# A two-block transformer on one core: index scores placed among the second queries' products, four last weight parts and a residual load moved, and the PSUM banks of some phases exchanged

## The chip, the cores and the metric

The kernel runs on one core of one Trainium2 chip. Its engines are TensorE (PE, with its weight loads shown apart as PEld), VectorE (DVE), ScalarE (ACT), GpSimd (POOL) and SyncE (SP, which only issues transfers here). The metric is the device time of one execution in microseconds, lower is better. A profile is a second kind of run: one execution recorded by the hardware profiler.

## The reference, cut to what matters

For 512 tokens of width 1024, all in float32, two blocks follow each other:

```python
# first block
z = rms_norm(x, norm1_g) @ w_in                       # glu_in, q, k, v, gate_logits
a = silu(rms_norm(conv31(a_val * sigmoid(a_gate)) + b, g));  y_a = a @ w_conv_out
o = mix over three dilated windows of softmax attention(q, k, v);  y_b = o @ w_attn_out
x = x + (g_a * y_a + g_b * y_b) @ w_out               # the residual is the input x
h = rms_norm(x, norm2_g)
u = conv3(h @ w_up);  x = x + (silu(u_gate) * u_val) @ w_down
# second block, first layer (sparse attention)
q, k, v, g, qi, wi, ki = split(x @ w_in_a)
rel = relu(einsum('qhd,sd->qhs', rope(qi), rope(ki)) * 64 ** -0.5)   # 8 index heads
score = einsum('qhs,qh->qs', rel, wi * 8 ** -0.5);  idx = top_k(score, 128)
x = layer_norm(ALPHA * x + (softmax attention over idx * silu(g)) @ w_out_a)
# second block, second layer (stick-breaking attention), then layer_norm
```

The index scores decide which keys a query sees: for each of three blocks of 128 queries (the first block needs no choice) and each of 8 index heads there is one product with a width of 256, 384 or 512 keys, a relu, and a weighted sum into a mask.

## The kernel before

**Weights.** All weight matrices stand in one stream of 231 slabs of 512 KB (`wstream`), in the order in which TensorE uses them (`PHASES`). A slab lies in one of four slots and is held in two parts, `W_HI` (rounded to the fast float32 format) and `W_LO` (the remainder). POOL does this (L422 to L440): for each slab it waits until the slab four places back is used up (`slab_done`), issues the load of `W_HI`, and then calls `remainder` for the slab before: negate `W_HI` into `W_LO` (L430), and issue a load that adds the original weights onto it (L433). `W_LO` is what TensorE waits for. For some early slabs ACT does the negation.

**Products.** Every product of 128 x 128 by 128 x 512 is three matmuls, high by high and two crosses (L451 to L453). A slab is 24 such matmuls. `f_phase` gives features by tokens, one PSUM bank per slab; `t_half` gives tokens by features, four slabs into four banks at once. Before it starts it waits until `tile_free` has counted enough tiles that were read out of PSUM. `tokens=` at the end of a phase makes the last two slabs of the half go token by token, so that both must be there when the first token's products run. `aside=` puts other work between slabs.

**Order of the work.** The program of each engine is written out by hand and every engine is strictly in order. TensorE goes through: the GLU projection (`glu`), the first q, k, v (`qkv`, L812), four early gate slabs, the rest of v, the convolution's output, attention "a" with the gate slabs as filling, `attn_out`, `w_out`, `up`, `down`, the index projection (`idx`), the second queries (`q2`, L853 to L859), and then as a block of its own: five turns of the index values (L868), and 24 score products (L877), where score `u` waits until the relu of score `u - 4` is done. After that come the second k and v (`kv2`), attention "b", `out_a`, and the last layer.

**Around the index scores.** ACT copies the index values out of PSUM, turns, copies the second queries (L945), copies the turned index values (L1205), and takes the 24 relus (L1212). DVE rotates the index values, and for each score adds the weighted relu onto `MASK` (L1747), then chooses the largest 128 of a row in 16 rounds, and rotates the second q and k.

**The residual of `w_out`.** `RESIDUAL` is a view of `GATE_B`. SP loads x into it again (L412) as one transfer of 2 MB, when all tiles of `attn_out` are free; DVE adds the products of `w_out` onto it.

## Time and profile before

| | us |
|---|---|
| median of 3 runs | 1651.69 (1646.33 to 1653.17) |
| the profiled execution | 1649.88 |
| its span | 1648.1 |
| TensorE busy in the span | 1561.9 (95%) |
| VectorE busy | 886.0 (54%) |
| ScalarE busy | 504.5 (31%) |
| GpSimd busy | 546.1 (33%) |
| weight stream, share of the 16 DMA engines | 68.7% |

The page cuts the span into 40 slices of some 41 us. TensorE is at 90% or more in nearly all of them. The transfers are at 80% to 90% of the DMA engines wherever TensorE goes through slabs without attention between them, and at 20% to 30% in the attention stretches. The chain of work that ended last lies on TensorE for 86% of the span. What is idle on TensorE adds up to some 5% in stretches of one to three microseconds.

### The profile page before, as it was taken

To read this page: it belongs to the slowest core of one execution; us is meant where nothing else is said; L and a number is where in the kernel's file an instruction comes from. 1 tells how busy PE (TensorE), PEld (TensorE's weight loads), DVE (VectorE), ACT (ScalarE), POOL (GpSimd) and SP (SyncE) were. 2 spreads that over 40 slices of the span, in tenths; PEclk is the share of its full clock that TensorE was granted. 3 is DMA by queue.
4 is the path that set the end of the run, shared out by engine and by line. 5 is a ranking of instruction groups with operands and counts; after the bars stand their busy time and mean duration, and the time that the engine had idled before them with its cause. 6 is when DMAs were issued, how large, how long until landed. Compare 5 with 4: busy or idle time off the path is not lost.

```text
span 1648.1 us, 19418 instructions
## 1 busy us (share of the span) xinstructions
PE 1561.9 (95%) x7634; PEld 1273.9 (77%) x7634; DVE 886.0 (54%) x1546; ACT 504.5 (31%) x1001; POOL 546.1 (33%) x662
## 2 busy tenths in 40 slices
PE   6999999899899999999999999999998989999997
PEld 5878888677778778888878787687776768888885
DVE  2899949256645144333400031895676261677675
ACT  4223333356541132222200011311676130444440
POOL 3222234311114344444444444144110334332321
PEclk9999999999999999999999999999999999999999
DMA  8989998623338978898888888398321758755655
GB/s 227 193 184 194 195 191 188 153 66 63 77 77 183 225 169 193 191 198 190 196 172 192 184 176 194 78 189 182 77 52 26 164 120 193 156 123 117 140 109 145
DMA packets 69274, 253.12 MB, mean 154 GB/s; under 512 B 7616, under 2 KB 7744, under 8 KB 69184
## 3 DMA queue, kind: packets, MB, share of 16 engines
q0 software_dynamic: 66528, 242.25, 68.7%
q1 hardware_dynamic: 2112, 7.53, 1.3%
q10 hardware_dynamic: 544, 2.10, 0.4%
q8 instruction: 61, 1.00, 0.3%
q14 instruction: 29, 0.24, 0.0%
HBM read 249.75 MB, written 2.10 MB: 153 GB/s over the span
## 4 chain that ended last, share of the span: by engine, by line
PE 86%; DVE 5%; DMA 3%; ACT 3%; issue 2%; POOL 0%; SPq 0%; DVEq 0%; ACTq 0%; POOLq 0%
PE PSUM L451 26%; PE PSUM L452 25%; PE PSUM L453 25%; DMA W_LO<-wstream 2%; PE PSUM L612 2%; PE PSUM L633 2%; PE PSUM L714 1%; PE PSUM L732 1%; PE PSUM L745 1%; PE PSUM L600 1%; DVE MASK L1747 1%; DMA SMALLS<-small 1%; DMA W_HI<-wstream 1%; PE PSUM L643 1%; ACT PROBS L968 0%
## 5 line engine op out<-in xcount | busy, mean ns | idle before, releaser
L439 POOL DMA_DIRECT2D W_HI<-wstream x231 | 129.5, 561 | 946.8 <-PE PSUM L453 946.3
L451 PE MATMUL PSUM<-X_HI,W_HI 128*128 128x512 f32 x872 | 350.0, 401 | 5.7 <-DVE X_LO L1332 2.6
L452 PE MATMUL PSUM<-X_LO,W_HI 128*128 128x512 f32 x872 | 342.1, 392 | 0.0
L453 PE MATMUL PSUM<-X_HI,W_LO 128*128 128x512 f32 x872 | 342.0, 392 | 0.0
L433 POOL DMA_DIRECT2D W_LO<-wstream x231 | 208.0, 900 | 105.2 <-POOL W_LO L430 84.2
L451 PE MATMUL PSUM<-W_HI,X_HI 128*128 128x512 f32 x544 | 213.8, 393 | 7.0 <-DMA W_LO<-wstream 2.7
L430 POOL TENSOR_SCALAR W_LO<-W_HI 128x1024 fp32r<-128x1024 f32 x195 | 210.3, 1079 | 23.1 <-DMA W_HI<-wstream 19.6
L452 PE MATMUL PSUM<-W_LO,X_HI 128*128 128x512 f32 x544 | 212.8, 391 | 0.0
L453 PE MATMUL PSUM<-W_HI,X_LO 128*128 128x512 f32 x544 | 212.7, 391 | 0.0
L451 PEld LDWEIGHTS PSUM<-X_HI,W_HI 128*128 128x128 f32 x872 | 165.0, 189 | 44.8 <-issue 7.5
L453 PEld LDWEIGHTS PSUM<-X_HI,W_LO 128*128 128x128 f32 x872 | 164.7, 189 | 35.8
L452 PEld LDWEIGHTS PSUM<-X_LO,W_HI 128*128 128x128 f32 x872 | 165.1, 189 | 32.0
L1597 DVE SCALAR_TENSOR_TENSOR CONV<-CONV_IN,SMALLS,CONV 128x512 f32<-128x512 f32 x240 | 159.4, 738 | 0.0
L1691 DVE SCALAR_TENSOR_TENSOR GATE_A<-PSUM,SMALLS,GATE_A 128x511 f32<-128x511 f32 x88 | 65.9, 749 | 143.2 <-ACT GATE_A L1173 141.6
L451 PEld LDWEIGHTS PSUM<-W_HI,X_HI 128*128 128x128 f32 x544 | 102.8, 189 | 31.8 <-DMA W_LO<-wstream 3.9
L453 PEld LDWEIGHTS PSUM<-W_HI,X_LO 128*128 128x128 f32 x544 | 102.8, 189 | 21.8
L452 PEld LDWEIGHTS PSUM<-W_LO,X_HI 128*128 128x128 f32 x544 | 102.8, 189 | 21.0
L1173 ACT ACTIVATE GATE_A<-PSUM,SMALLS 128x512 f32<-128x512 f32 x44 | 34.3, 779 | 166.2 <-PE PSUM L453 165.5
L968 ACT ACTIVATE PROBS<-PROBS,soft_stats 128x128 f32<-128x128 f32 (+3 forms) x128 | 70.7, 557 | 39.3 <-DVE soft_stats L1397 39.2
L1355 DVE TENSOR_TENSOR GATE_B<-PSUM,GATE_B 128x512 f32<-128x512 f32 x16 | 10.5, 687 | 130.8 <-PE PSUM L453 130.8
L1093 ACT ACTIVATE W_LO<-W_HI 128x1024 fp32r<-128x1024 f32 x36 | 38.2, 1062 | 138.9 <-DMA W_HI<-wstream 138.9
L451 PE MATMUL PSUM<-W_HI,FFN_HI 128*128 128x512 f32 x176 | 69.3, 394 | 3.9 <-DVEq L1695 2.5
(225 smaller groups left out, 2465.8 us busy)
## 6 DMA issues: line engine op xcount, KB each, us to landing
W_HI<-wstream POOLq DMA_DIRECT2D x231, 512.0 KB, 3.9
W_LO<-wstream POOLq DMA_DIRECT2D x231, 512.0 KB, 5.7
GATE_A<-x SPq DMA_DIRECT2D x4, 512.0 KB, 5.8
GATE_B<-x SPq DMA_DIRECT2D x1, 2048.0 KB, 16.5
NORM_GAINS<-lnv ACTq DMA_DIRECT2D x2, 1024.0 KB, 5.9
out<-GATE_B SPq DMA_DIRECT2D x3, 512.0 KB, 2.6
CONST<-consts SPq DMA_DIRECT2D x1, 968.0 KB, 10.7
out<-GATE_B SPq DMA_DIRECT2D x2, 256.0 KB, 2.0
```

The source lines that it names most:

```text
L430: pool.tensor_scalar(W_LO[:, r, :], W_HI[:, r, :].bitcast(F32), -1.0, 0.0, ALU.mult, ALU.add)\
L433: pool.dma_start(W_LO[:, r, :], wstream[n], accum_op=ALU.add).then_inc(w_lo_in[r], 16)
L439: pool.dma_start(W_HI[:, n % SLOTS, :], wstream[n]).then_inc(w_hi_in[n % SLOTS], 16)
L451: pe.matmul(o, lh, rh, start=start, stop=False)
L452: pe.matmul(o, lh, rl, start=False, stop=False)
L453: return pe.matmul(o, ll, rh, start=False, stop=stop)
L612: mm = pe.matmul(PSUM[:, SCORE_BANK[q % 2][h], 0:n], l[d, par, 0, c], r[d, par, 1, 0:n], start=part == 0, stop=part == 2)
L968: act.activation(p, p, ACT.Exp, scale=-1.0, bias=soft_stats[:, 0, q, h:h + 1], accum_out=soft_stats[:, 1, q, h:h + 1]).then_inc(sem(f"{a}_ ...
L1093: act.activation(W_LO[:, r, :], W_HI[:, r, :].bitcast(F32), ACT.Copy, scale=-1.0).then_inc(sem("w_neg_act"), 1)
L1173: act.activation(FFN_CONV[:, 2 * m + v, :], PSUM[:, 2 * m + v, :], ACT.Identity, scale=SMALLS[:, bass.ds(i * 12 + (S_AT["fw"].start + (2 * ...
L1597: dve.scalar_tensor_tensor(acc, src, w, acc, ALU.mult, ALU.add).then_inc(step, 1)
L1691: ins = dve.scalar_tensor_tensor(FFN_CONV[:, b, d:], PSUM[:, b, 0:SEQ - d], w, FFN_CONV[:, b, d:], ALU.mult, ALU.add)
```

## The change

It has five parts.

1. *Index scores.* The turn of the index keys and weights, the five turns of the rotated index values, and the 24 scores are put between the slabs of `q2`. The first half of `q2` has one of the turns before each of its slabs 1, 2 and 3; the first four scores stand between the halves; the other 20 stand in fours before the second to sixth of the eight k tiles of the second half. Both halves of `q2` now use banks 4 to 7; turns and scores use banks 0 to 3. ACT takes the index copies before the second queries.
2. *Last parts first.* For the last slab of `w_out`, `down` and `out_a`, POOL does the `remainder` before it waits for the next slot and issues the next slab's `W_HI`.
3. *Residual.* x is loaded again into the place of the first values (`QKV[:, 2]`), in eight column pieces, each as soon as attention "a" has split that piece of the values (`a_v_lo`). DVE reads x there and writes to `RESIDUAL` as before.
4. *Banks.* `qkv` starts in banks 4 to 7 (it was 0 to 3), and the phases up to `conv_out` have their banks exchanged likewise. `glu` ends in banks 0 to 3. The wait for all tiles of `glu` at the start of `t_loop` is gone.
5. *`down`.* Its first half, in banks 4 to 7, waits for four tiles fewer of `up`, which uses banks 0 to 3 alone.

```diff
+INDEX_TURNS = ((TT, 0), (0, 1), (1, 2), (2, 3), (3, 0))
+EARLY_REMAINDER = [SLAB_END[name] - 1 for name in ("w_out", "down", "out_a")]
+        X_AGAIN = QKV[:, 2, :, :]
...
-            sp.wait_ge(tile_free, TILE0["attn_out"] + 8)
-            sp.dma_start(RESIDUAL, x.rearrange("(t p) d -> p t d", p=P)).then_inc(sem("res_in"), 16)
+            for k in range(KT):
+                sp.wait_ge(sem("a_v_lo"), k + 1)
+                sp.dma_start(X_AGAIN[:, :, o_part(k)], x[:, o_part(k)].rearrange("(t p) d -> p t d", p=P))\
+                    .then_inc(sem("res_in"), 16)
...
             for n in range(SLABS):
+                if n - 1 in EARLY_REMAINDER:
+                    remainder(n - 1)
                 if n >= SLOTS:
                     pool.wait_ge(slab_done, n - SLOTS + 1)
                 pool.dma_start(W_HI[:, n % SLOTS, :], wstream[n]).then_inc(w_hi_in[n % SLOTS], 16)
-                if n:
+                if n and n - 1 not in EARLY_REMAINDER:
                     remainder(n - 1)
...
-            def t_loop(name, turns):
+            def t_loop(name, turns, first_bank=0):
                 s0, t0 = SLAB0[name], TILE0[name]
-                pe.wait_ge(tile_free, t0)
                 for i in range(0, turns):
                     for c in range(2):
-                        t_half(4 * c, s0 + 8 * i + 4 * c, KT, X_HI, X_LO, t0 + 8 * i + 4 * c - 4)
+                        t_half((first_bank + 4 * c) % 8, s0 + 8 * i + 4 * c, KT, X_HI, X_LO, t0 + 8 * i + 4 * c - 4)
...
-            t_loop("qkv", 2)
-            t_half(0, SLAB0["qkv"] + 16, KT, X_HI, X_LO, TILE0["qkv"] + 12)
+            t_loop("qkv", 2, first_bank=4)
+            t_half(4, SLAB0["qkv"] + 16, KT, X_HI, X_LO, TILE0["qkv"] + 12)
...
-            t_phase("down", ..., FT, FFN_HI, FFN_LO, first_bank=4,
-                    tokens="down_token", aside=(4, lambda: turn_residual(range(0, 4), 4, TILE0["down"] + 4)))
+            t_phase("down", ..., FT, FFN_HI, FFN_LO, first_bank=4, ahead=4,
+                    tokens="down_token", aside={4: lambda: turn_residual(range(0, 4), 4, TILE0["down"] + 4)})
...
+            def turn_index(some):
+                pe.wait_ge(sem("i_roped"), TT + 1)
+                for k, bank in some:
+                    pe.wait_ge(tile_free, turned0 + (k == TT - 1))
+                    for t in range(TT):
+                        src = INDEX_Q[:, t, k * P:(k + 1) * P] if k < TT else INDEX_K[:, t, :]
+                        mm = pe.transpose(PSUM[:, bank, t * P:(t + 1) * P], src, ident)
+                    mm.then_inc(sem("i_turned"), 1)
+            def index_scores(step):
+                if step == 0:
+                    give(pe, "i_scores")
+                    pe.wait_ge(tile_free, turned0 + 5)
+                for u in range(4 * step, 4 * step + 4):
+                    qb, h = u // IH + 1, u % IH
+                    r = slice(h % 2 * HD, h % 2 * HD + HD)
+                    need(pe, "i_relu", u - 3)
+                    pe.matmul(PSUM[:, u % 4, 0:(qb + 1) * P], INDEX_Q_T[r, h // 2, qb * P:(qb + 1) * P],
+                              INDEX_K_T[r, 0:(qb + 1) * P], start=True, stop=True).then_inc(sem("i_scores"), 1)
+            def scores_beside(k):
+                if 0 < k < 3 * IH // 4:
+                    index_scores(k)
+            t_half(4, s0, KT, X_HI, X_LO, i0 + 4,
+                   aside={1: turn_weights, 2: lambda: turn_index(INDEX_TURNS[:4]), 3: lambda: turn_index(INDEX_TURNS[4:])})
+            index_scores(0)
+            t_half(4, s0 + 4, KT, X_HI, X_LO, t0 + 4, scores_beside)
...
+            def second_queries(c):
+                act.wait_ge(slab_done, SLAB0["q2"] + 4 * c + 4)
+                for t in range(TT):
+                    act.activation(QKV[:, 0, t, c * SEQ:(c + 1) * SEQ], PSUM[:, 4 + t, :], ACT.Copy).then_inc(tile_free, 1)
...
+                old = X_AGAIN[:, t, c * SEQ:(c + 1) * SEQ] if name == "w_out" else r
+                dve.tensor_tensor(r, PSUM[:, bank, :], old, ALU.add).then_inc(tile_free, 1)
...
-            dve.wait_ge(sem("res_in"), 16)
+            dve.wait_ge(sem("res_in"), 16 * KT)
```

**TensorE from the turn of the index keys and weights (`INDEX_KW_T`) to the second k and v.** Before, with the waits of each row in brackets; the left-out rows are products of `q2`:

```order
L858 MATMUL PSUM<-CONST,INDEX_KW_T 128x72 [waits tile_free]
L858 MATMUL PSUM<-CONST,INDEX_KW_T 128x72 x3
L451 MATMUL PSUM<-W_HI,X_HI 128x512 [waits w_lo_in3,tile_free]
...
L868 MATMUL PSUM<-CONST,INDEX_Q 128x128 [waits i_roped,tile_free]
L868 MATMUL PSUM<-CONST,INDEX_Q 128x128 x15
L868 MATMUL PSUM<-CONST,INDEX_K 128x128 x4
L877 MATMUL PSUM<-INDEX_K_T,INDEX_Q_T 128x256 [waits tile_free]
L877 MATMUL PSUM<-INDEX_K_T,INDEX_Q_T 128x256 x3
L877 MATMUL PSUM<-INDEX_K_T,INDEX_Q_T 128x256 [waits i_relu] x4
L877 MATMUL PSUM<-INDEX_K_T,INDEX_Q_T 128x384 [waits i_relu] x8
L877 MATMUL PSUM<-INDEX_K_T,INDEX_Q_T 128x512 [waits i_relu] x8
L451 MATMUL PSUM<-W_HI,X_HI 128x512 [waits tile_free,w_lo_in3,i_relu]
```

The same place in the changed kernel, from the last turn on; each "..." stands for 11 or 23 matmuls of `q2`:

```order
L883 MATMUL PSUM<-CONST,INDEX_Q 128x128 [waits tile_free,i_roped]
L883 MATMUL PSUM<-CONST,INDEX_Q 128x128 x3
L464 MATMUL PSUM<-W_HI,X_HI 128x512 [waits w_lo_in2]
...
L895 MATMUL PSUM<-INDEX_K_T,INDEX_Q_T 128x256 [waits tile_free]
L895 MATMUL PSUM<-INDEX_K_T,INDEX_Q_T 128x256 x3
L464 MATMUL PSUM<-W_HI,X_HI 128x512 [waits w_lo_in3,tile_free]
...
L895 MATMUL PSUM<-INDEX_K_T,INDEX_Q_T 128x256 [waits i_relu] x4
...
L895 MATMUL PSUM<-INDEX_K_T,INDEX_Q_T 128x384 [waits i_relu,w_lo_in0]
L895 MATMUL PSUM<-INDEX_K_T,INDEX_Q_T 128x384 [waits i_relu] x3
...
L895 MATMUL PSUM<-INDEX_K_T,INDEX_Q_T 128x512 [waits i_relu] x4
```

The block of 20 turns and 24 scores behind the last product of `q2` has gone up between the products, and the first product of the second half now waits for `tile_free`: for the copies of the first half, whose banks it takes.

**ACT at the same place**, before:

```order
L1197 ACTIVATE INDEX_KW<-PSUM 128x288
L945 ACTIVATE QKV<-PSUM 128x512 x8
L1205 ACTIVATE INDEX_Q_T<-PSUM 128x512 x4
L1205 ACTIVATE INDEX_K_T<-PSUM 128x512
L1212 ACTIVATE INDEX_RELU<-PSUM 128x256 x8
```

and in the changed kernel:

```order
L1224 ACTIVATE INDEX_KW<-PSUM 128x288
L1230 ACTIVATE INDEX_K_T<-PSUM 128x512
L1230 ACTIVATE INDEX_Q_T<-PSUM 128x512 x4
L1235 ACTIVATE QKV<-PSUM 128x512 x4
L1244 ACTIVATE INDEX_RELU<-PSUM 128x256 x8
L1244 ACTIVATE INDEX_RELU<-PSUM 128x384 x8
L1244 ACTIVATE INDEX_RELU<-PSUM 128x512 x8
L1235 ACTIVATE QKV<-PSUM 128x512 x4
```

The relus stand between the copies of the two halves of the second queries.

**POOL at the last slab of `w_out`** (slot 3, as `w_hi_in3` says), before:

```order
L439 DMA W_HI<-wstream 128x1024 [waits slab_done]
L430 TENSOR_SCALAR W_LO<-W_HI 128x1024 [waits w_hi_in2]
L433 DMA W_LO<-wstream 128x1024 [waits w_neg]
L439 DMA W_HI<-wstream 128x1024 [waits slab_done]
L430 TENSOR_SCALAR W_LO<-W_HI 128x1024 [waits w_hi_in3]
L433 DMA W_LO<-wstream 128x1024 [waits w_neg]
```

and in the changed kernel:

```order
L452 DMA W_HI<-wstream 128x1024 [waits slab_done]
L441 TENSOR_SCALAR W_LO<-W_HI 128x1024 [waits w_hi_in2]
L444 DMA W_LO<-wstream 128x1024 [waits w_neg]
L441 TENSOR_SCALAR W_LO<-W_HI 128x1024 [waits w_hi_in3]
L444 DMA W_LO<-wstream 128x1024 [waits w_neg]
L452 DMA W_HI<-wstream 128x1024 [waits slab_done] x2
L441 TENSOR_SCALAR W_LO<-W_HI 128x1024 [waits w_hi_in0]
```

The negation and the second load of slot 3 no longer stand behind a wait for `slab_done`; the next slab's `W_HI` stands behind them.

## Rows read from the trace of the kernel before

**Rows 1.** The page, part 1: busy time and share of the span of each engine.

```profile
PE 1561.9 (95%) x7634; PEld 1273.9 (77%) x7634; DVE 886.0 (54%) x1546; ACT 504.5 (31%) x1001; POOL 546.1 (33%) x662
```

**Rows 2.** Waits of TensorE on weights: line, waited for, us in total, times, longest.

```profile
PE PSUM L451 <- DMA W_LO<-wstream: 5.6, 5, 1.4
```

**Rows 3.** Windows, TensorE: start:end, length, busy us (instructions), granted clock, DMA share, GB/s.

```profile
453.00:480.00 27.00, 23.16 (x131) 0.94 0.19 40
536.00:552.00 16.00, 14.65 (x64) 1.00 1.00 279
600.00:820.00 220.00, 220.00 (x972) 1.00 0.89 193
828.20:832.60 4.40, 4.40 (x14) 0.61 0.84 156
981.98:1026.60 44.62, 44.12 (x197) 1.00 0.87 188
1026.60:1048.26 21.66, 16.23 (x69) 0.98 0.32 68
1048.26:1054.30 6.04, 6.03 (x14) 0.50 0.00 0
```

**Rows 4.** Timeline, index block: start us, us, engine, line, operation, [idle before <- releaser].

```profile
1026.80 2.06 ACT L945 ACTIVATE QKV<-PSUM 128x512 f32<-128x512 f32 x4 [20.20 <-PE PSUM L453]
1028.91 1.97 PE L868 MATMUL PSUM<-CONST,INDEX_Q 128*128 128x128 f32 x16 [2.16 <-ACT QKV L945]
1030.72 0.60 PE L868 MATMUL PSUM<-CONST,INDEX_K 128*128 128x128 f32 x4
1032.21 0.73 PEld L877 LDWEIGHTS PSUM<-INDEX_K_T,INDEX_Q_T 64*128 64x128 f32 x8 [1.14 <-ACT INDEX_K_T L1205]
1032.21 13.76 PE L877 MATMUL PSUM<-INDEX_K_T,INDEX_Q_T 64*128 64x256 f32 x48 [0.90 <-ACT INDEX_K_T L1205]
...
1048.27 0.80 PE L451 MATMUL PSUM<-W_HI,X_HI 128*128 128x512 f32 x1 [2.29 <-ACT INDEX_RELU L1212]
```

**Rows 5.** Groups by form, 1026 to 1049: busy us, mean ns, idle before.

```profile
L877 PE MATMUL PSUM<-INDEX_K_T,INDEX_Q_T 64*128 64x512 f32 x16 | 6.6, 641 | 0.1
L1747 DVE SCALAR_TENSOR_TENSOR MASK<-INDEX_RELU,INDEX_W,MASK 128x512 f32<-128x512 f32 x6 | 4.5, 751 | 0.6
```

**Rows 6.** Timeline, from the index keys' turn to their last copy.

```profile
1003.77 0.41 PE L858 MATMUL PSUM<-CONST,INDEX_KW_T 72*128 72x72 f32 x4
1004.22 0.41 ACT L1197 ACTIVATE INDEX_KW<-PSUM 128x288 f32<-128x288 f32 x1 [21.45 <-PE PSUM L858]
1008.51 0.28 DVE L1729 COPY INDEX_K<-INDEX_KW 128x256 f32<-128x256 f32 x1
```

**Rows 7.** Timeline: first product of `qkv`; of `down`; DVE before attention "b".

```profile
110.66 0.50 PE L451 MATMUL PSUM<-W_HI,X_HI 128*128 128x512 f32 x1 [1.53 <-ACT CONV_IN L1103]
...
827.90 0.50 PE L451 MATMUL PSUM<-W_HI,FFN_HI 128*128 128x512 f32 x1 [2.49 <-DVEq L1695]
...
1147.13 0.69 DVE L1423 SCALAR_TENSOR_TENSOR GATE_A<-GATE_TANH,PSUM 128x512 f32<-128x512 f32 x1 [13.47 <-ACT GATE_TANH L1014]
```

**Rows 8.** Timeline of POOL at the last slab of `down`.

```profile
929.87 0.56 POOL L439 DMA_DIRECT2D W_HI<-wstream  x1 [2.47 <-PE PSUM L453]
...
935.31 0.56 POOL L439 DMA_DIRECT2D W_HI<-wstream  x1 [2.45 <-PE PSUM L453]
937.38 0.90 POOL L433 DMA_DIRECT2D W_LO<-wstream  x1 [0.43 <-POOL W_LO L430]
```

**Rows 9.** Line L439, the load issued at 929.87 and then that at 1310.13: landing.

```profile
DMA to landing us min/median/max: 3.8/3.8/3.8
...
DMA to landing us min/median/max: 5.1/5.1/5.1
```

**Rows 10.** Chain of waits, 530 to 946: the longest weight transfers on it.

```profile
535.68 9.73 DMA W_LO<-wstream
...
937.38 5.74 DMA W_LO<-wstream
```

More of the change, by code:

```diff
@@ L74 @@
     ("glu", 16), ("qkv", 20), ("early", 4), ("v_tail", 4), ("conv_out", 8), ("gates", 12), ("attn_out", 8), ("w_out", 8),
-    ("up", 2 * FT), ("down", 8), ("idx", 6), ("q2", 8), ("x_idx", 5), ("kv2", 16), ("g2", 8), ("out_a", 8),
+    ("up", 2 * FT), ("down", 8), ("idx", 6), ("x_idx", 5), ("q2", 8), ("kv2", 16), ("g2", 8), ("out_a", 8),
     ("qk_b", 2), ("v_b", 8), ("stick", 3 * PAIRS - 2), ("out_b", 8),
@@ L481, in x_ready, with f_phase @@
                 return lambda k: pe.wait_ge(sem("x_lo"), X0[name] + max(k, least) + 1)
-            def f_phase(name, ready, hi=lambda k: X_HI[:, k, :], lo=lambda k: X_LO[:, k, :], upper=0, wide=False):
+            def f_phase(name, ready, hi=lambda k: X_HI[:, k, :], lo=lambda k: X_LO[:, k, :], upper=0, wide=False, first_bank=0):
                 s0, t0 = SLAB0[name], TILE0[name]
@@ L540, in t_half @@
                 for n in slabs or range(kts // 2 - (2 if tokens else 0)):
-                    if aside and n == aside[0]:
-                        aside[1]()
+                    if aside and n in aside:
+                        aside[n]()
                     slab(n)
@@ L851, in _ @@
             mm.then_inc(slab_done, 1)
-            s0, t0, i0 = SLAB0["q2"], TILE0["q2"], TILE0["idx"]
-            t_half(4, s0, KT, X_HI, X_LO, i0 + 4)
-            pe.wait_ge(tile_free, i0 + 5)
-            for t in range(TT):
-                mm = pe.transpose(PSUM[:, 1, t * n:(t + 1) * n], INDEX_KW_T[0:n, t * P:(t + 1) * P],
-                                  CONST[0:n, C_AT["ident"].start:C_AT["ident"].start + n])
-            mm.then_inc(sem("i_kw"), 1)
-            t_half(0, s0 + 4, KT, X_HI, X_LO, t0)
@@ L863, in _ @@
-            pe.wait_ge(tile_free, TILE0["x_idx"])
-            pe.wait_ge(sem("i_roped"), TT + 1)
-            for k in range(TT + 1):
-                for t in range(TT):
-                    src = INDEX_Q[:, t, k * P:(k + 1) * P] if k < TT else INDEX_K[:, t, :]
-                    mm = pe.transpose(PSUM[:, k, t * P:(t + 1) * P], src, ident)
-                mm.then_inc(sem("i_turned"), 1)
-            give(pe, "i_scores")
-            pe.wait_ge(tile_free, TILE0["x_idx"] + 5)
-            for u in range(3 * IH):
-                qb, h = u // IH + 1, u % IH
-                r = slice(h % 2 * HD, h % 2 * HD + HD)
-                need(pe, "i_relu", u - 3)
-                pe.matmul(PSUM[:, u % 4, 0:(qb + 1) * P], INDEX_Q_T[r, h // 2, qb * P:(qb + 1) * P],
-                          INDEX_K_T[r, 0:(qb + 1) * P], start=True, stop=True).then_inc(sem("i_scores"), 1)
+            s0, t0, i0, turned0 = SLAB0["q2"], TILE0["q2"], TILE0["idx"], TILE0["x_idx"]
@@ L1142, in _ @@
             for t in range(TT):
[L1143 removed]
+                act.activation(QKV[:, 2, t, SEQ:], PSUM[:, t, :], ACT.Copy).then_inc(tile_free, 1)
             act.wait_ge(sem("q_ms"), 1)
```

38 lines of the change are left out of this document (21 added, 17 removed).

## The prediction

> **What bounds the kernel now.** I read the page's busy times first: TensorE is busy for 1561.9 us, 95% of the span [rows 1], the other engines for 54% at most. So time is won only where TensorE stands still or runs slowly. Next the windows. In the 220 us of `up`, TensorE gets through 972 matmuls without a gap [rows 3], 220/972 = 0.226 us for each: that is the pace, and a slab of 24 takes 5.43 us. The weight stream keeps that pace with the DMA engines at 0.89 [rows 3]. Then the waits of TensorE: a wait shown as idle X costs X + 0.16, because a matmul is drawn 0.39 us long and the next would have come 0.23 after its start. Last the timelines around the waits that the change touches. The reader should see there that all of them are short, except one place: between the last product of the second queries and the first of the second k and v, 21.66 us pass [rows 3] with 20 turns and 24 small scores in them, and behind it 14 matmuls run at granted clock 0.50, the level of 1.2 GHz [rows 3].
>
> **Part 1, index scores.** From the start of `q2` to the start of `kv2` it was 1048.27 - 981.98 = 66.3 us [rows 3, 4]. In the changed order the same work is:
> - 8 slabs, 192 matmuls at 0.226: 43.5.
> - The turn of keys and weights, 4 short matmuls of 0.41 together [rows 6], with the change of operand: 0.7.
> - 20 turns: before, from 1028.91 to 1030.72 + 0.60 [rows 4], 2.4.
> - 24 scores. Before they took 13.76 [rows 4], since from the fifth on each waits for a relu, which waits for DVE. A group of four that waits for nothing has its 8 weight loads in 0.73 [rows 4], so about 1.0 with its last product; wider scores in proportion, 1.5 and 2.0 (the mean of one matmul goes up to 641 ns at 512 [rows 5]). Two groups of each width: 9.0. The bounds are 6 x 0.73 = 4.4 from the loads alone and the 13.8 of before. I take 9.0, because the wait for the relu should be over: between two groups lie 12 products, 2.7 us, so a group comes each 3.7 to 4.7 us, and DVE needs 4 x 0.751 = 3.0 [rows 5] at the widest, 3.5 with its gaps.
> - One new wait. The second half takes the banks of the first, so it waits for ACT's four copies. Before, that same wait, ahead of the turns, was from 1026.60 to 1028.91 [rows 3, 4], 2.3. The first four scores now fill 1.0 of it: 1.3 left. Behind it on TensorE's queue stands everything; nothing else is late by it, since the stream is ahead.
> - The turns need the rotated index keys. From the end of the small turn to the last copy of the keys it was 1008.79 - 1004.18 = 4.6 us [rows 6]; one slab, 5.43, now lies between. That wait is covered by 0.8 us; if POOL or DVE is late, it costs up to about 1.
>
> Sum 43.5 + 0.7 + 2.4 + 9.0 + 1.3 = 56.9, against 66.3: 9.4 us less. With the bounds of the scores it is 4.6 to 14.0.
>
> The 14 matmuls at 0.50 took 6.04 [rows 3] instead of 3.2. They came right after the sparse scores and a wait of 2.29 [rows 4], and the changed order has no such stretch: 2.9 less. Bounds: 0 if the clock falls elsewhere instead, 2.9 if not. I take 2.9.
>
> The Trainium skill ("TensorE: Matmul & The Clock Gate", "Part 1: The HAM clock gate (the "warmup" mystery)") says that the clock follows how busy the array has been and that the monitor is free-running, so the same kernel can pay a different number of slow matmuls from run to run. The trace agrees with the first; of the second it shows one run only. By it the clock's terms here (2.9, and 1.2 below) may turn up at another place, and the time would be some 4 us higher.
>
> DVE begins its choice of the largest some 17 us earlier and TensorE reaches attention "b" some 12 earlier. In the trace DVE, done with the rotations behind the choice, stands idle for 13.47 us before its first work of that attention [rows 7], so it does not become the bound.
>
> **Part 4, banks.** The first product of `qkv` waited for ACT's last copy out of `glu`: 1.53 + 0.16 = 1.7 [rows 7]. It now writes to the other four banks. Next late would be the weights of the following slabs; they come by the same queues as before, 1.7 us nearer to their use, and four slots are in flight. Gain 1.7; bounds 0 and 1.7.
>
> **Part 5, `down`.** 2.49 + 0.16 = 2.65 [rows 7]. The tiles that it now waits for were counted before the last slab of `up` was done; the first FFN values it needs are long there. Right behind, 14 matmuls took 4.40 at clock 0.61 [rows 3] instead of 3.2: another 1.2. Together 3.85; bounds 0 and 3.85, and I take the upper, since nothing else is named for that moment.
>
> **Parts 2 and 3, weights.** TensorE waits five times on `W_LO`, 5.6 us in all [rows 2], four of them about 1.4, each worth 1.5. One is at the start of the second part of `w_out`: there a `W_LO` took 9.73 us instead of 5.7 [rows 10], beside the residual's 2 MB, with the DMA engines at 1.00 [rows 3]. The load now happens in attention "a", where the last pieces fall into a stretch at 0.19 [rows 3]. Gain 1.5, hidden by that free share; bounds 0 and 1.5.
>
> The Trainium skill ("DMA: Bandwidth & Descriptors", "Anatomy of one DMA — SWDGE (gpsimd) path") gives some 2 us fixed for a transfer whatever its size, so eight transfers would pay it eight times. No row shows a piece of this shape; at attention's free share the sum would be the same.
>
> The other three are last slabs, needed 4 us early because two slabs go token by token. For `down`: W_HI was issued at 929.87 and landed 3.8 later [rows 8, 9], 933.7; POOL can then negate (1.06, and 0.43 to the issue) and issue at 935.2 instead of 937.38 [rows 8]. With 5.7 [rows 10] it lands at 940.9 instead of 943.1; TensorE wants it at 941.6. All 1.6 go. For `w_out` the same reckoning leaves 0.8 to spare: 1.5. For `out_a` the W_HI took 5.1 [rows 9], so the start comes only about 0.9 earlier: 0.9 of 1.5. Sum 4.0, bounds 0 and 4.6. The price is that the next W_HI is issued about 0.9 later; its remainder waits for a later slab anyway, so nothing is late by it.
>
> **Sum.** 9.4 + 2.9 + 1.7 + 3.85 + 1.5 + 4.0 = 23.35. The profiled execution took 1649.88, so its like would be 1626.5. The median of the runs is 1.8 above it: 1651.69 - 23.35 = 1628.3. I forecast 1628.
>
> **Rivals.**
> - *The scores keep their waits.* If relu and DVE still set the pace inside the groups, TensorE's slab products now wait behind them: scores 13.8 instead of 9.0, and the sparse stretch may still pull the clock down: 4.8 + 2.9 less won, 1636. For it: in-order queues, and ACT has the copies of the queries ahead of the first relus. Against it: 2.7 us of products between groups. 0.12.
> - *The weight stream becomes the bound.* The waits also let the stream fill its slots; without them W_LO is late elsewhere. For it: DMA share 0.87 to 0.89 at full pace, and 1.00 near the residual. Against it: 972 matmuls in a row without a wait. Then only the residual's wait, the three last parts and part of the rest stay won, some 7: 1645. 0.09.
> - *A wait only changes its name* in parts 2 to 5 (another copy or transfer ends at the same moment), and part 1 alone works: 1651.7 - 12.3 = 1639.4. Against it: the reckonings above have 0.7 us and more to spare at most places. 0.04.
> - *Slower: the clock falls within `q2`.* Turns and scores, which use the array thinly, now stand among the full products. If they pull the granted clock to 1.2 GHz, the products around them pay: 6.04/14 = 0.43 us [rows 3] instead of 0.226, 0.2 each. From some 100 slow products on (20.5 of gain without the 2.9, over 0.2) the change loses; if it held over 6 of the 8 slabs, 144 x 0.2 = 29, and 9 more for the scores, it would be 1631.2 + 38 = 1669. Against it: before, the clock fell only behind 14 us of scores with nothing between. 0.03.
>
> The Trainium skill's page on the clock gate (same section) would rather speak against this last one, as full products keep the array busy.
>
> **How the numbers follow.** Forecast 0.72, its own range 1620 to 1635: it takes in the scores' lower bound and a clock term more or less, and the runs before lay 7 us apart. Rivals 0.12, 0.09, 0.04, 0.03. About 0.5% (8 us) is what a measurement of this kernel can tell from no change. Forecast, first and third rival are faster by more than that: 0.88; I say 0.87. The second is within it: 0.09, 0.10 with an odd mishap. Slower 0.03. Range for 8 in 10: 1619 to 1640, which leaves out the second and fourth rival and the tail of the first.
>
> **What would show it.** In the changed profile: no stretch of turns and scores alone; `kv2` starts some 57 us after `q2`; TensorE's waits on `INDEX_RELU` are gone or under 0.5 each, and one of about 1.3 on the copy of the queries stands between the halves; no row of waits on `CONV_IN` at `qkv` nor on DVE at `down`; waits on `W_LO` down from 5.6 to about 1; the granted clock 1.00 after the scores. Wrong would be: score groups with waits of 1 us and more, new waits on `W_LO` within slabs in `q2` or `qkv`, or a low clock inside `q2`.

## The result and the profile after

| | before, us | after, us |
|---|---|---|
| median of the runs | 1652.26 (1646.33 to 1653.17, 4 runs) | 1625.78 (1617.07 to 1627.42, 4 runs) |
| the profiled execution | 1649.88 | 1617.07 |
| its span | 1648.1 | 1615.3 |

The ratio is 0.9842, with an interval of 0.9803 to 0.988. The change makes the kernel 26 us faster, 20 to 33 by the interval; forecast were 1628 and a range of 1619 to 1640. A fifth run of the changed kernel, 1628.14, is on record outside this median; with it the median would be 1627.1. The profiled execution of after is also its fastest run, 8.7 below the median. What is read from its trace must therefore be told apart from its luck; the later runs help with that.

The busy times of the page of after, for [rows 1]:

```profile
PE 1545.1 (96%) x7634; PEld 1263.4 (78%) x7634; DVE 887.3 (55%) x1546; ACT 502.9 (31%) x1001; POOL 546.3 (34%) x662
```

TensorE has the same 7634 matmuls and is busy for 16.8 us less, since more of them run at the higher clock and the scores are no longer drawn out by waits. The span is 32.8 shorter, so the other 16 us are idle time that is gone.

TensorE's waits in after (line, waited for, us in total, times, longest), for [rows 2] and those of [rows 4, 7]:

```profile
PE PSUM L464 <- ACT QKV L972: 2.2, 1, 2.2
PE PSUM L464 <- DVE INVERSE L1469: 2.2, 1, 2.2
...
PE PSUM L464 <- ACT QKV L1235: 1.1, 1, 1.1
```

No row for `W_LO`, `CONV_IN`, `INDEX_RELU` or DVE's queue is left. New is the wait of 1.1 on L1235, the copies of the second queries between the halves.

Windows of TensorE in after (start:end, length, then busy us and count for PE, PEld, DVE, ACT, POOL, granted clock, DMA share, GB/s): the second part of `w_out`, the head of `down`, the two halves of `q2`, and the head of the second k and v. They answer to [rows 3].

```profile
536.00:545.00 9.00, 9.00 (x41) 7.48 (x40) 0.00 (x0) 0.00 (x0) 3.73 (x5) 1.00 0.86 174
815.54:819.94 4.40, 4.40 (x21) 3.66 (x20) 3.11 (x5) 2.79 (x5) 2.50 (x3) 1.00 0.88 202
966.10:992.79 26.69, 25.61 (x129) 20.87 (x127) 12.87 (x34) 5.78 (x12) 11.70 (x14) 1.00 0.81 175
992.79:1023.69 30.90, 30.89 (x137) 21.18 (x138) 20.38 (x40) 9.68 (x24) 8.44 (x10) 1.00 0.57 123
1023.69:1029.73 6.04, 6.04 (x28) 5.03 (x27) 6.04 (x19) 2.07 (x4) 2.59 (x4) 1.00 0.84 181
```

In 4.40 us at the head of `down` TensorE now does 21 matmuls, and did 14; in 6.04 us at the head of the second k and v it does 28, and did 14. The clock is at its higher level in both, and inside `q2` too.

The timeline of after (start us, us, engine, line, operation, [idle before <- releaser]): the end of the index keys' way, as [rows 6]; the wait between the halves; then one group of four scores at 384, and one at 512 with the products behind it, as [rows 4].

```profile
971.57 0.41 PE L872 MATMUL PSUM<-CONST,INDEX_KW_T 72*128 72x72 f32 x4
976.33 0.28 DVE L1763 COPY INDEX_K<-INDEX_KW 128x256 f32<-128x256 f32 x1
977.34 0.60 PE L883 MATMUL PSUM<-CONST,INDEX_K 128*128 128x128 f32 x4
...
992.79 0.50 PE L464 MATMUL PSUM<-W_HI,X_HI 128*128 128x512 f32 x1 [1.09 <-ACT QKV L1235]
...
999.75 1.56 PE L895 MATMUL PSUM<-INDEX_K_T,INDEX_Q_T 64*128 64x384 f32 x8
...
1013.48 1.99 PE L895 MATMUL PSUM<-INDEX_K_T,INDEX_Q_T 64*128 64x512 f32 x8
1014.64 2.07 ACT L1244 ACTIVATE INDEX_RELU<-PSUM 128x512 f32<-128x512 f32 x4 [2.79 <-PE PSUM L895]
1015.27 3.32 DVE L1781 SCALAR_TENSOR_TENSOR MASK<-INDEX_RELU,INDEX_W,MASK 128x512 f32<-128x512 f32 x4 [1.47 <-ACT INDEX_RELU L1244]
1015.39 0.50 PE L464 MATMUL PSUM<-W_HI,X_HI 128*128 128x512 f32 x1
...
1016.20 0.40 PE L464 MATMUL PSUM<-W_HI,X_HI 128*128 128x512 f32 x1
```

The last copy of the keys ends at 976.61, 4.6 after the end of the small turn, as before, and the turns begin at 977.34 with no wait: some 0.7 to spare. In the group of scores DVE is done at 1018.6, ACT at 1016.7. Both now idle ahead of a group (2.79 and 1.47). Before, TensorE's weight loads had stood still for them: from the fifth score on, by 0.3 to 0.4 us ahead of most scores. Here is one such row of before, and then the loads of the group at 1013.48 of after, which wait for no relu ("issue" stands for no releaser that the profile shows):

```profile
1043.41 0.29 PEld L877 LDWEIGHTS PSUM<-INDEX_K_T,INDEX_Q_T 64*128 64x128 f32 x2 [0.43 <-ACT INDEX_RELU L1212]
```
```profile
1013.48 0.30 PEld L895 LDWEIGHTS PSUM<-INDEX_K_T,INDEX_Q_T 64*128 64x128 f32 x4 [0.35 <-issue]
```

POOL at the last slab of `down` in after, for [rows 8]:

```profile
915.75 0.55 POOL L452 DMA_DIRECT2D W_HI<-wstream  x1 [2.49 <-PE PSUM L466]
...
919.69 1.04 POOL L441 TENSOR_SCALAR W_LO<-W_HI 128x1024 fp32r<-128x1024 f32 x1 [0.96 <-DMA W_HI<-wstream]
921.14 0.89 POOL L444 DMA_DIRECT2D W_LO<-wstream  x1 [0.41 <-POOL W_LO L441]
921.73 0.87 POOL L452 DMA_DIRECT2D W_HI<-wstream  x1
```

The `W_LO` load is issued 5.4 us after its `W_HI`; before, it was 7.5.

**Where the time went, stretch by stretch.** Each length is from the first product of one stretch to that of the next, or to one close behind it that is the same in every kernel (the second product of `attn_out` and of `up`, the eleventh of `out_a`), read from the timelines (us; "low" is how much of a stretch was granted 1.2 GHz). Attention a and b are the stretches up to `attn_out` and from `g2` to `out_a`.

| | to `qkv` | att. a (low) | `attn_out` to second part of `w_out`, and on to `up` | `up` to `down` | `down` (low) | `q2` | second k, v (low) | att. b (low) | `out_a` |
|---|---|---|---|---|---|---|---|---|---|
| before | 88.9 | 181.2 (23.9) | 55.7 + 40.6 | 241.8 | 124.3 (3.4) | 66.3 | 92.4 (6.0) | 149.5 (6.8) | 52.9 |
| after | 87.2 | 178.4 (17.1) | 54.2 + 38.6 | 239.2 | 120.8 (0) | 57.6 | 89.5 (0) | 146.3 (0) | 51.1 |
| gain | 1.7 | 2.8 | 1.5 + 2.0 | 2.65 | 3.5 | 8.7 | 2.9 | 3.2 | 1.75 |

Without the two attention stretches, where the change has no work to save, the gains add up to 24.7; forecast 23.35. The attentions give 6.0 more, the start of the program 1.55, the last layer 0.4: 32.8 in all.

### The profile page after: what moved, and what is told of

It reads as the page before. It is cut to its first block, busy times and chain, and to the rows that moved or that the text cites. A ratio compares the mean times of both kernels' runs of the same rounds, so it can differ in the third digit from the quotient of the medians.

```text
span 1615.3 us, 19427 instructions
## 1 busy us (share of the span) xinstructions
PE 1545.1 (96%) x7634; PEld 1263.4 (78%) x7634; DVE 887.3 (55%) x1546; ACT 502.9 (31%) x1001; POOL 546.3 (34%) x662
## 4 chain that ended last, share of the span: by engine, by line
PE 90%; DVE 5%; ACT 3%; issue 1%; DMA 1%; SPq 0%; DVEq 0%; ACTq 0%
PE PSUM L464 27%; PE PSUM L465 27%; PE PSUM L466 27%; PE PSUM L624 2%; PE PSUM L645 2%; PE PSUM L726 1%; PE PSUM L744 1%; PE PSUM L757 1%; PE PSUM L612 1%; DMA SMALLS<-small 1%; PE PSUM L655 1%; PE PSUM L895 0%; ACT PROBS L995 0%; ACT QKV L1258 0%; ACT X_HI L1260 0%
## 5 line engine op out<-in xcount | busy, mean ns | idle before, releaser
L645 PE MATMUL PSUM<-CONST,PROBS 128*128 128x128 f32 x320 | 48.4, 288 | 21.1 <-DVE PT_LO L1443 17.5
```

The lines of the kernel that those rows point to most:

```text
L645: mm = pe.transpose(PSUM[:, bank, at + kb * P:at + (kb + 1) * P], PROBS[:, h, k:k + P], ident)
```

## The experiments

All ratios are against the kernel before, run on the same chip. Medians of the kernel before were 1651.64, 1649.47, 1652.09 and 1651.04 in the four rounds of experiments. The ratios are those on record; they are not quotients of two medians and differ from them by up to 0.0023 (e5: 0.9842, the medians give 0.9865).

**e1_only_index: part 1 alone.** The kernel before, with part 1 of the change only. Against the changed kernel, in short (the residual, the banks and the wait of `down` are those of before as well):

```diff
-EARLY_REMAINDER = [SLAB_END[name] - 1 for name in ("w_out", "down", "out_a")]
...
             def t_loop(name, turns):
+                pe.wait_ge(tile_free, t0)
```

> The kernel before with part 1 alone (index turns and scores among the slabs of q2, ACT's order with them). Theory: the parts add up, so this wins part 1's share: q2 to kv2 in 57 to 58 us instead of 66.3, no low clock behind it, 12.3 us less, about 1640. The waits at qkv, down and on the four weight parts stay as they were (1.5, 2.5 and four of about 1.4). Rival: the parts help each other (the stream is ahead only when the other waits are there), and this alone wins under 8 us.

Measured: 1645.85 (1639.88 to 1648.1, 10 runs), ratio 0.9954 [0.9939, 0.9969]. That is 5.8 us by the medians and 7.6 by the ratio, where 12.3 were expected: the rival's size, under 8. TensorE's waits on `W_LO` are 8.4 us in 6 in this execution, where before had 5.6 in 5; the longest, 2.95 behind `down`, has low clock behind it. But `q2` also took 59.95, not 57.58. The timeline shows the difference at the head of the second k and v:

```profile
1043.43 0.47 PE L454 MATMUL PSUM<-W_HI,X_HI 128*128 128x512 f32 x1 [2.20 <-issue]
```

The row names no releaser, but `t_loop` begins with a wait for all copies of the second queries, which the change takes out. The prediction had read its removal as a matter of `qkv` alone.

**e2_no_index: all but part 1.** The turns, scores and banks of `q2` as before.

```diff
-            t_half(4, s0, KT, X_HI, X_LO, i0 + 4, aside={1: turn_weights, 2: ..., 3: ...})
-            index_scores(0)
-            t_half(4, s0 + 4, KT, X_HI, X_LO, t0 + 4, scores_beside)
+            t_half(4, s0, KT, X_HI, X_LO, i0 + 4)
+            ...
+            t_half(0, s0 + 4, KT, X_HI, X_LO, t0)
+            ...the 20 turns and 24 scores in one block
```

> The changed kernel with part 1 undone and parts 2 to 5 kept. Theory: the time of the changed kernel plus 12.3, about 1638, with the waits of 2.2, 0.9 and 2.3 around the turns and scores back and 14 matmuls at half clock behind them. Rival: the weights' parts and banks are worth less than 11 us by themselves, and this stands within 6 us of the kernel before.

Measured: 1637.61 (1635.18 to 1638.33), ratio 0.9912 [0.9891, 0.9933]. The block's waits are back:

```profile
PE PSUM L464 <- ACT INDEX_RELU L1226: 2.3, 1, 2.3
...
PE PSUM L882 <- ACT QKV L959: 2.2, 1, 2.2
```

and so is the lower clock behind it, to 0.72 over the first 6 us of the second k and v:

```profile
1039.37:1045.41 6.04, 6.04 (x19) 4.84 (x20) 5.69 (x15) 0.00 (x0) 0.00 (x0) 0.72 0.00 0
```

`q2` took 67.66 and the stretch behind it 91.19: 10.1 + 1.7 more than in after. On top of the other parts, part 1 brings 11.8. In this execution TensorE was also granted the lower clock for 6.8 us within `q2`, right behind the wait of 2.2 on the copies (from 1019.8), where before had 0.8; so the 10.1 holds a piece of clock. The other four parts alone bring some 14 by the medians and 13.1 by the table above, where 11.05 were forecast.

**e3_scores_block: turns moved, scores not.**

```diff
-            index_scores(0)
-            t_half(4, s0 + 4, KT, X_HI, X_LO, t0 + 4, scores_beside)
+            t_half(4, s0 + 4, KT, X_HI, X_LO, t0 + 4)
+            for step in range(3 * IH // 4):
+                index_scores(step)
```

> The changed kernel with the turns where it has them, but all 24 scores in one block behind the second half of q2. Theory: the gain of part 1 lies in the scores and not in the turns, so this gives nearly all of it back: the scores take 13.8 again, TensorE waits 2.3 for the last relu, the wait in the middle of q2 is 2.2 instead of 1.1, and the clock falls behind the block for 14 matmuls. 11 us over the changed kernel, about 1637. Rival: moving the turns and ACT's copies off the end was the gain, and this costs under 6.

Measured: 1633.95 (1632.63 to 1637.14), ratio 0.9895 [0.9874, 0.9917]. `q2` took 67.08 and the stretch behind 91.21, 9.5 + 1.8 more than in after. So in the traces nearly all of part 1 is the scores; the moved turns alone bring some 0.6. The wait of 2.3 on `INDEX_RELU` is back, and the wait between the halves grows to 2.2, since no scores stand ahead of it; here too 3.4 us of low clock follow it. The medians give less than the traces: 8.2 and 6.7 us over the two of the changed kernel (1625.78, and 1627.23 in e5), where 11 were expected, and 3.7 under e2. The intervals of e2 and e3 overlap, so the share of the turns rests on the traces.

**e9_index_no_wait: part 1 and the wait at the second k and v.** e1 with one line changed:

```diff
             def t_loop(name, turns):
-                pe.wait_ge(tile_free, t0)
+                if name == "qkv":
+                    pe.wait_ge(tile_free, t0)
```

> As e1_only_index (the kernel before with the index scores moved between the second queries' slabs, and nothing else), but the wait for all copies of the second queries at the head of the second keys and values (in `t_loop`) is taken out, as it is in the changed kernel; the other use of `t_loop` keeps it. Theory: this wait is what e1 lost. Then the stretch from the second queries to the second keys and values is 57.6 us as in the changed kernel, not 59.95, and the time falls by a further 2.4 us and by what the clock then keeps, to some 1641 (part 1 worth 8.7 + 2.9 against the kernel before, less what the run has of low clock elsewhere). Rival: e1's shortfall was only the weights' low parts and the clock of that execution; then the stretch stays near 60 and the time at e1's 1646.

Measured: 1642.02 (1638.19 to 1645.35, 6 runs), ratio 0.9933 [0.9906, 0.9959]; `q2` took 57.58, as in after. The head of the second k and v has no wait, and its window reads as that of after:

```profile
1038.89:1044.93 6.04, 6.04 (x28) 5.02 (x27) 6.04 (x19) 2.07 (x4) 2.58 (x4) 1.00 0.85 187
```

Part 1 with this line brings 11.1 by the ratio, the 11.8 of e2 from the other side.

**e10_wait_kept: the changed kernel with that wait.**

```diff
             def t_loop(name, turns, first_bank=0):
+                if name == "kv2":
+                    pe.wait_ge(tile_free, t0)
```

> The changed kernel, with that one wait put back ahead of the second keys and values. Theory: the stretch grows from 57.6 by 2.4 us to 60.0, since nothing of TensorE's stands any more between the last product of the second queries and this wait, and the copies end 2.2 us and more behind that product; the time is 2.4 above the changed kernel's, about 1628, or more if the gap takes the clock with it. Rival: the first half of the keys and values waits for the copies of its own banks anyway (2.2 us at L972 in the changed kernel), so the wait moves but is not added: the stretch grows, and the one behind shrinks by as much; the time stays at 1626.

Measured: 1629.73 (1629.23 to 1630.23, 4 runs), ratio 0.9857 [0.983, 0.9884]. `q2` took 59.94, 2.36 more, and the stretch behind it 89.55, no less. ACT's copies and the wait:

```profile
1028.91 2.06 ACT L1237 ACTIVATE QKV<-PSUM 128x512 f32<-128x512 f32 x4 [7.18 <-PE PSUM L466]
```
```profile
1031.07 0.47 PE L464 MATMUL PSUM<-W_HI,X_HI 128*128 128x512 f32 x1 [2.20 <-issue]
```

TensorE starts 0.10 after the last of ACT's four copies ends: the copies are what it waits for. The removed line is worth 2.4 us, and only together with part 1: in before, the turns and scores stand between the last product and this wait, and e2, which lacks the wait, has the same 2.3 on `INDEX_RELU` there.

**e11_waits_back: the waits of parts 4 and 5.**

```diff
             def t_loop(name, turns, first_bank=0):
+                if name == "qkv":
+                    pe.wait_ge(tile_free, t0)
...
-            t_phase("down", ..., first_bank=4, ahead=4,
+            t_phase("down", ..., first_bank=4,
```

> The changed kernel with the two waits of parts 4 and 5 back: the first product of `qkv` waits again for all tiles of `glu`, and the first half of `down` for all tiles of `up` (both keep their banks). Theory: each wait costs its idle time and 0.16, so the stretch ahead of `qkv` grows by 1.7 us and that ahead of `down` by 2.65; behind `down`'s wait the clock drops again to a mean of about 0.6 over 14 products, 0.8 to 1.2 more. Together 5.2 to 5.6 in the profile and some 1631 to 1632 in the median. Rival: the clock term has nothing to do with the wait; then it is 4.35, with the granted clock at 1.00 behind the wait of `down`, and 1630.

Measured: 1633.57 (1631.07 to 1638.18, 6 runs), ratio 0.99 [0.9878, 0.9922]. The stretch to `qkv` grows by 1.9, that to `down` by 2.64, `down` itself by 1.76. Timeline and window at the head of `down`:

```profile
824.47 0.50 PE L464 MATMUL PSUM<-W_HI,FFN_HI 128*128 128x512 f32 x1 [2.50 <-DVEq L1731]
...
826.13 0.63 PE L464 MATMUL PSUM<-W_HI,FFN_HI 128*128 128x512 f32 x1
```
```profile
824.80:829.20 4.40, 4.40 (x14) 3.45 (x13) 2.29 (x4) 1.23 (x2) 0.48 (x1) 0.61 0.90 169
```

The window is that of before to the digit, 14 matmuls in 4.40 at 0.61. In all four kernels that have this wait (before, e1, e9, e11), the clock fell to its lower level behind it; in the ten executions that do not, it never did there. So the clock term belongs to the wait. The clock costs 1.8 there, more than the 0.8 to 1.2 expected. The profile says 6.3 for the two waits with it, the medians 6.3 to 7.8 (against e5 and after).

**e6_late_parts: part 2 undone.**

```diff
-EARLY_REMAINDER = [SLAB_END[name] - 1 for name in ("w_out", "down", "out_a")]
+EARLY_REMAINDER = []
```

> The changed kernel with part 2 undone: the last weight parts of w_out, down and out_a are issued behind the next slab's load. Theory: three waits on W_LO of about 1.4 come back and nothing else moves: 4.5 us more. Rival: part 2 only changed the name of a wait, under 1 us.

Measured: 1632.04 (1631.43 to 1636.19), ratio 0.9885 [0.9858, 0.9912]. The waits on the three slabs are back, at their places:

```profile
565.96 0.50 PE L464 MATMUL PSUM<-W_HI,X_HI 128*128 128x512 f32 x1 [1.10 <-DMA W_LO<-wstream]
...
934.09 0.50 PE L464 MATMUL PSUM<-W_HI,FFN_HI 128*128 128x512 f32 x1 [1.27 <-DMA W_LO<-wstream]
...
1303.97 0.50 PE L464 MATMUL PSUM<-W_HI,O_HI 128*128 128x512 f32 x1 [1.12 <-DMA W_LO<-wstream]
```

The three stretches grow by 1.40, 1.56 and 1.54: 4.5 in all, for 4.0 forecast. The medians say 4.8 to 6.3.

**e7_late_residual: part 3 undone.** The 2 MB of x again in one load to `RESIDUAL`, behind the second half of `attn_out`.

```diff
-            for k in range(KT):
-                sp.wait_ge(sem("a_v_lo"), k + 1)
-                sp.dma_start(X_AGAIN[:, :, o_part(k)], ...).then_inc(sem("res_in"), 16)
+            sp.wait_ge(tile_free, TILE0["attn_out"] + 8)
+            sp.dma_start(RESIDUAL, x.rearrange("(t p) d -> p t d", p=P)).then_inc(sem("res_in"), 16)
```

> The changed kernel with part 3 undone: x is loaded again in one transfer of 2 MB when attn_out's tiles are free. Theory: one W_LO takes 9 to 10 us again and TensorE waits 1.3 to 1.4 for it, 1.5 us more and nothing else. Rival: without the wait of before at qkv and elsewhere the stream has less in hand here, and the wait is longer, 3 us and more.

Measured: 1627.03 (1624.97 to 1633.61), ratio 0.9856 [0.9828, 0.9883]. Its chain of waits again has a long transfer, and TensorE waits behind it:

```profile
532.53 9.40 DMA W_LO<-wstream
```
```profile
541.97 0.50 PE L462 MATMUL PSUM<-W_HI,X_HI 128*128 128x512 f32 x1 [1.01 <-DMA W_LO<-wstream]
```

In after, the three `W_LO` loads issued between 529.5 and 540.4 took 5.6 to 7.3. In this execution the stretch is 1.2 longer, and the one up to `up` 2.5, with a second wait on `W_LO` of 0.60 at 565.98 and 3.1 us of low clock in it, which no other kernel has there. Whether these two belong to the late load is open. The median does not tell part 3 from nothing: 1627.0 against 1625.8 and 1627.2. Its 1.2 is thus seen in traces only. As for the price of eight loads instead of one: SP, not GpSimd, issues them; in after each landed 2.6 to 6.4 us behind its issue, the last issued at 468.4, long before DVE needs x for `w_out`.

**e5_again: the changed kernel once more.**

> The changed kernel once more, unchanged. Theory: its runs differ by where the granted clock falls, so the profile has the same waits as the first one to 0.1 us, and where the span differs by several us, the stretches at 1.2 GHz differ in number and in sum by about twice that. Rival: the difference between runs lies in transfers or waits.

Measured: 1627.23 (1621.02 to 1627.99, 4 runs), ratio 0.9842 [0.981, 0.9874]. All lengths of the table are those of after within 0.1, but for one `W_LO` wait of 1.54 at 945.86, behind `down`, and 3.4 us of low clock in attention b (147.98 instead of 146.27). The spans of these two executions of one kernel differ by 3.95: 1.8 with the wait, 1.7 in attention b, 0.4 in the last layer. So the expectation that all waits would be the same missed one, and its rival holds for near half of the difference. Such a wait at that place also stood in e8 (1.37) and e11 (1.28), in three of the ten executions with part 2 and in none of the four without. It may be a price of the early last part, whose next `W_HI` is issued later than it was; that was not tested, and three of ten don't settle it.

**e4_by_tile: the copies waited for one by one.** The second half of `q2` waits for each tile and not for four, and the first gate slab of attention b for one tile fewer.

```diff
+                            if by_tile and k == 0:
+                                pe.wait_ge(tile_free, free - TT + t + 1)
...
-                        slab_quarter(n, part, s0, (SLAB_BANK, OUT_BANK)[n], t0)
+                        slab_quarter(n, part, s0, (SLAB_BANK, OUT_BANK)[n], t0 + n - 1)
```

> The changed kernel, but the second half of q2 waits for ACT's copies bank by bank instead of for all four, and the first gate slab of attention b waits for the third copy and not the fourth. Theory: a copy takes 0.5 us and the three matmuls of a bank 0.68, so the wait of 1.1 between the halves of q2 goes to under 0.3, and the wait of 2.25 before the gate slab falls by 0.5: 1.5 us less in all, about 1624, at the edge of what can be told. Rival: the scores between the halves already cover it and the first copy is the late one, so nothing is won.

Measured: 1625.11 (1621.51 to 1626.12), ratio 0.9835 [0.9814, 0.9857]. The wait of 1.1 between the halves is gone, that on L975 is 1.8 instead of 2.2; `q2` took 56.41 and the stretch behind it 88.96, 1.66 less together. The medians don't tell it from the changed kernel.

**e8_eights: scores in groups of eight.**

```diff
-                if 0 < k < 3 * IH // 4:
-                    index_scores(k)
+                for step in {2: (1, 2), 4: (3, 4), 6: (5,)}.get(k, ()):
+                    index_scores(step)
```

> The changed kernel with the 20 scores of the second half in groups of 8, 8 and 4 (before k tiles 2, 4 and 6) instead of five groups of 4. Theory: in a group of 8 the second four wait for relus that go at DVE's pace, 0.6 to 0.86 a score: waits on the relu appear, 1.4 us for each group of 8, 3 us more in all. Rival: the products between groups do not matter, TensorE waits in neither, under 1 us.

Measured: 1624.37 (1622.46 to 1630.05), ratio 0.9833 [0.9803, 0.9863]; `q2` took 57.89, only 0.3 more. TensorE's weight loads do wait for the relus in the second four, but briefly:

```profile
1005.93 1.22 PEld L895 LDWEIGHTS PSUM<-INDEX_K_T,INDEX_Q_T 64*128 64x128 f32 x8 [0.44 <-ACT INDEX_RELU L1244]
...
1013.36 3.85 PE L895 MATMUL PSUM<-INDEX_K_T,INDEX_Q_T 64*128 64x384 f32 x16
1014.31 4.39 ACT L1244 ACTIVATE INDEX_RELU<-PSUM 128x384 f32<-128x384 f32 x8 [4.85 <-PE PSUM L895]
```

This eight is four at 384 and four at 512 (the row names the first's shape) and took 3.85, where the two fours take 1.56 + 1.99 = 3.55 in after. The loss of 0.3 in each of two eights is half made up for, by two entries into a group that are saved. So the size of a group matters little; what matters is that ACT and DVE get the time of some products between groups. The expectation of 3 us had taken the pace of the block for that of any row of more than four.

**e12_tile_eights: e4 and e8 together.**

> The changed kernel with both of e4 and e8: the copies of the second queries are waited for tile by tile, and the last 20 scores stand in groups of eight, eight and four, not in fours. Theory: e8 lost only 0.3 us in the stretch of the second queries, since eight scores wait for the relus by 0.4 and 0.5 and save the entries of two groups; e4 won 1.66 there and behind it. So the stretch is 56.7 us, the one behind it 89.0, the profile 1.3 below the changed kernel's but for the clock elsewhere, and the median 1624 to 1625, which can't be told from 1626. Rival: the eights hold ACT longer, so that its copies of the second half come later; then the wait at the second keys and values grows and the two don't add up.

Measured: 1623.32 (1618.63 to 1624.62, 4 runs), ratio 0.983 [0.9807, 0.9854]: the lowest median of all, against 1625.78 and 1627.23 of the changed kernel, with intervals that overlap. `q2` took 56.73 and the stretch behind it 88.96, 1.3 less than in after, as forecast. It is a step of the size of what can't be told, seen in the trace and not proved in the time.

## Why the prediction was right

**Its sum.** With what the profile measured:

| term | forecast | measured | seen in |
|---|---|---|---|
| part 1, `q2` | 9.4 | 8.7 | after; e2 10.1, e3 9.5, both with low clock in `q2` |
| clock behind the scores | 2.9 | 2.9 | after; 1.7 in e2, e3 |
| part 4, `qkv` | 1.7 | 1.7 | after; 1.9 in e11 |
| part 5, wait and clock | 2.65 + 1.2 | 2.65 + 1.8 | after, e11 |
| part 3 | 1.5 | 1.5 | after; 1.2 in e7 |
| part 2, `down`, `w_out`, `out_a` | 1.6 + 1.5 + 0.9 | 1.6 + 1.4 + 1.5 | e6; 2.0 for `w_out`, 1.75 for `out_a` in after |

**Part 1.** `q2` took 57.58, forecast 56.9. The first half with its scores and its wait was 26.69, where the working gives 21.7 + 0.7 + 2.4 + 1.0 + 1.3 = 27.1. The second was 30.90, of which 96 products are 21.7 and five groups of scores 9.2; the working had 8.0. A group of four takes 1.13, 1.56 and 1.99 at the three widths and was priced at 1.0, 1.5 and 2.0, which makes some 0.2 over the five; and left out is that the first product behind a group comes late as well (1015.39 to the next of its line 1016.20, 0.81 where 0.68 is the pace), another 0.65. The rest of 0.3 was not traced. So the scores were too cheap by 1.2 and the wait and turns too dear by 0.4. The chain of reasons held: relu and DVE catch up beneath the products. Its step "a group comes each 3.7 to 4.7 us, and DVE needs 3.0" was true (4.0 to 4.9, and 3.3 to 3.4) and stricter than it had to be, as the eights show.

**What it did not see.** Part 1 is worth 8.7 in `q2` only with the wait of `t_loop` gone, which belongs to part 4 and was priced there for `qkv` alone. Kept, that wait costs 2.4 (e10), and part 1 brings 7.6 by e1's ratio instead of e9's 11.1; the rest of that difference lies within the intervals. The sum came out right because both are in the change. Of the steps that it named for `q2`, none had the end of the second half in it: there, too, a bank is handed on.

**Part 2.** `out_a` was too low, 0.9 for 1.5. The step that failed is that its `W_HI` would take the 5.1 of [rows 9] again. In after that load took 4.1 us, and `W_LO` is issued 5.6 behind it, not 6.6:

```profile
1279.43 0.55 POOL L452 DMA_DIRECT2D W_HI<-wstream  x1 [2.48 <-PE PSUM L466]
...
1285.04 0.88 POOL L444 DMA_DIRECT2D W_LO<-wstream  x1 [0.41 <-POOL W_LO L441]
```

In e12 it took 4.9, and there a piece of the wait was left, as the working would have it (stretch 51.96 instead of 51.11):

```profile
1297.96 0.50 PE L464 MATMUL PSUM<-W_HI,O_HI 128*128 128x512 f32 x1 [0.44 <-DMA W_LO<-wstream]
```

So the mechanism was right, and the size depends on a transfer's time that differs by 0.8 between executions.

**Clock.** The two clock terms were said to be those of a wait or a sparse stretch right ahead, and the runs bear that out place by place. For the lower clock at the second k and v: it stood there or in `q2` in before, e2 and e3, which have the block of scores, and in none of the eleven without. Which part of that block does it, the thin scores or the wait of 2.3 at their end, no run separates; a wait of 2.2 alone at the same place did not in two executions (e1, e10), but a wait of that length brought it elsewhere in some executions and not in others (last section). The text had these terms "may turn up at another place, and the time would be some 4 us higher". They did not, at these places. But the attention stretches do spread over the 14 executions: from 17.1 to 27.3 us at the lower level in a, 0 to 13.7 in b, with the same instructions. Windows of both, of after and then of e8:

```profile
305.20:483.60 178.40, 159.88 (x929) 128.80 (x930) 101.88 (x253) 95.63 (x248) 32.23 (x39) 0.95 0.38 87
1113.13:1259.40 146.27, 133.64 (x842) 106.81 (x843) 90.50 (x248) 86.41 (x237) 20.99 (x25) 1.00 0.30 65
```
```profile
305.68:487.75 182.07, 163.13 (x929) 131.31 (x930) 101.86 (x253) 95.59 (x248) 32.24 (x39) 0.93 0.39 86
1119.75:1271.41 151.66, 139.56 (x843) 111.50 (x843) 90.51 (x248) 86.59 (x237) 20.99 (x25) 0.95 0.30 63
```

The same work (929 matmuls, and 842 or 843) took 3.7 and 5.4 us longer in e8. Both kernels contain the whole change, so this is not its doing, and it is of the size of the 8.7 us by which the profiled execution of after beat its own median. The mean granted clocks on record fit: 0.990 in that execution and 0.984 to 0.986 in the other four, by which they had some 12 to 19 us more at the lower level; at 0.4 to 0.5 us each, read from the attention stretches, that is an estimate of 5 to 9 us. The 6.0 us of the attentions in the table above must not be booked as gain. The forecast did not, since it had taken its sum place by place and its level from the median. The medians leave room as well: they are 26.5 us apart in the first comparison and 22.2 in that of e5, on either side of the 23.35.

**The rivals.** *Scores keep their waits* would have shown as a wait on the relu in each group of four; there is none, and even the eights of e8 have 0.5. *The weight stream becomes the bound*: there is no wait on `W_LO` in after; in other kernels with parts 2 and 3 single ones of 0.4 to 1.5 come (e2, e5, e8, e11, e12; two in e8, 2.1 together), so a trace of it is real, 0 to 2 us, not 16. *A wait only changes its name* is refuted by e11 and e6, where each undone part gives back its own wait in full; what is left of it is the wait behind `down` in three executions of ten (e5), and part 3, which the medians can't tell. *The clock falls within `q2`*: it is granted 1.00 there in both halves.

## What to carry over

Short work that makes another engine hurry (scores with a relu and an add behind each) is best cut into small groups between long work of the same engine; the other engines need their time between groups more than the groups need to be small (eights cost 0.3 us more than fours, one block 9.5). When an order is changed, look for every wait that stood behind the moved block: it was free while the block covered it, and here one line of it was worth 2.4 us of 11. And before a gain is read off two profiles, take out the stretches in which the change does nothing: here they held 6 of 33 us.
